# Gate vectors of a two-layer diffusion block: partition sums and spread over partitions in one matrix product instead of two

## What is computed

```
for layer in range(2):
    mod_l = silu(c) @ w_mod[layer] + b_mod[layer]            # latent vectors
    sh1, sc1, g1, sh2, sc2, g2 = split(mod_l, 6)             # 1024 each
    mod_c = silu(c_ctx) @ w_mod[layer] + b_mod[layer]        # context vectors
    y_l, y_c = mixer(LN(x)*(1+sc1)+sh1, ..., w_in, w_out)    # four head groups
    x = post_norm(x, g1 * y_l)                               # LN(ALPHA*x + g1*y)
    x = post_norm(x, g2 * swiglu(LN(x)*(1+sc2)+sh2, w_gate_up, w_down))
    # the same for ctx with cg1, cg2, in layer 0 only
```

## Time and profile before

| | |
|---|---|
| runs of the kernel before | 1733.26, 1728.02, 1728.55 us |
| median | 1728.55 us |
| span of the profiled execution | 1726.8 us |
| PE busy | 1648.3 us (95%) |
| POOL, DVE, ACT busy | 853.3, 826.3, 454.1 us |
| granted TensorE clock, 40 slices | 9 in each of them |

### The profile page before, as it was taken

The page is one execution under the profiler, slowest core; times in us unless marked ns, Lnnn a source line. Parts: engine busy times, 40 slices in busy tenths (PEclk is TensorE's granted clock), DMA queues, the critical chain, the costliest instruction groups (busy, mean ns, idle before and its releaser), DMA issues. The chain is left out here.

```text
span 1726.8 us, 23654 instructions
## 1 busy us (share of the span) xinstructions
PE 1648.3 (95%) x9480; PEld 1391.7 (81%) x9480; DVE 826.3 (48%) x1236; ACT 454.1 (26%) x945; POOL 853.3 (49%) x840
## 2 busy tenths in 40 slices
PE   6999999999899999999999999999999999999997
PEld 4877866767899987899998788786768888688885
DVE  4353254647772415444445684635477421520048
ACT  5511465423500021100003164126433300210021
POOL 4443143623464443544444581523475577587772
PEclk9999999999999999999999999999999999999999
DMA  9212043311353312244642120210013542233321
GB/s 359 76 50 73 2 130 129 109 57 53 98 159 98 110 43 67 64 144 120 198 159 76 67 74 25 73 50 8 26 52 98 147 146 92 92 98 98 98 85 49
DMA packets 157010, 161.98 MB, mean 94 GB/s; under 512 B 6382, under 2 KB 111966, under 8 KB 156646
## 3 DMA queue, kind: packets, MB, share of 16 engines
q1 hardware_dynamic: 136566, 121.40, 22.8%
q10 hardware_dynamic: 20336, 39.08, 6.9%
HBM read 158.36 MB, written 2.10 MB: 93 GB/s over the span
## 5 line engine op out<-in xcount | busy, mean ns | idle before, releaser
L675 POOL TENSOR_SCALAR ring_hi<-stage 128x512 fp32r<-128x512 f32 x352 | 247.9, 704 | 621.4 <-PE ps L745 595.0
L678 POOL TENSOR_TENSOR ring_lo<-stage,ring_hi 128x512 fp32r<-128x512 f32 x352 | 490.0, 1392 | 29.4
L743 PE MATMUL ps<-act_hi,ring_hi 128*128 128x384 f32 (+2 forms) x1088 | 379.9, 349 | 0.0
L745 PE MATMUL ps<-act_hi,ring_lo 128*128 128x384 f32 (+2 forms) x1088 | 378.3, 348 | 0.0
L744 PE MATMUL ps<-act_lo,ring_hi 128*128 128x384 f32 (+2 forms) x1088 | 378.2, 348 | 0.0
L743 PE MATMUL ps<-ring_hi,act_hi 128*128 128x512 f32 (+1 forms) x700 | 280.7, 401 | 11.6 <-DVE act_lo L1872 5.4
L745 PE MATMUL ps<-ring_hi,act_lo 128*128 128x512 f32 (+1 forms) x700 | 273.3, 390 | 0.0
L744 PE MATMUL ps<-ring_lo,act_hi 128*128 128x512 f32 (+1 forms) x700 | 273.1, 390 | 0.0
L745 PEld LDWEIGHTS ps<-act_hi,ring_lo 128*128 128x128 f32 x1088 | 204.6, 188 | 13.2
L743 PEld LDWEIGHTS ps<-act_hi,ring_hi 128*128 128x128 f32 x1088 | 204.7, 188 | 13.0
L744 PEld LDWEIGHTS ps<-act_lo,ring_hi 128*128 128x128 f32 x1088 | 204.7, 188 | 12.9
(11 more groups left out here) (258 smaller groups left out, 2123.3 us busy)
## 6 DMA issues: line engine op xcount, KB each, us to landing
stage<-in_w_gate_up_dram SPq DMA_DIRECT2D x88, 512.0 KB, 5.1
mod_stage<-in_w_mod_dram ACTq DMA_DIRECT2D x56, 512.0 KB, 4.4
stage<-in_w_in_dram SPq DMA_DIRECT2D x18, 1024.0 KB, 5.0
stage<-in_w_down_dram SPq DMA_DIRECT2D x16, 1024.0 KB, 4.9
stage<-in_w_mod_dram SPq DMA_DIRECT2D x12, 1024.0 KB, 5.2
start_mod<-in_w_mod_dram SPq DMA_DIRECT2D x8, 1024.0 KB, 12.3
stage<-in_w_down_dram SPq DMA_DIRECT2D x8, 768.0 KB, 4.4
stage<-in_w_out_dram SPq DMA_DIRECT2D x16, 256.0 KB, 4.5
```

The lines of the kernel that those rows point to most:

```text
L675: nc.gpsimd.tensor_scalar(hi_, stage[:, par, j * 512:(j + 1) * 512], 1.0, 0.0, ALU.mult, ALU.add).then_inc(w_hi, 1)
L678: nc.gpsimd.tensor_tensor(lo_, stage[:, par, j * 512:(j + 1) * 512], hi_.bitcast(F32), ALU.subtract).then_inc(w_ready, 1)
L743: nc.tensor.matmul(o, a_hi, b_hi, start=first, stop=False)
L745: return nc.tensor.matmul(o, a_lo, b_hi, start=False, stop=last)
```

## The change

The accumulators are no longer summed into rows first. `mod_gates` multiplies 128 x 128 ones (`ones` read 128 times) with the accumulator itself: each of the 128 output rows is then the sum over partitions. For layer 0's modG a column `pick_gate` takes the place of the ones; it picks the stream's partial sums and row 2, into which SP brings the bias. For the others DVE adds the bias, once the last part is in, to one partition (0 or 32) of the accumulator (L2062 of the new kernel), from `bias_row`, which SP fills behind units 1 and 2 of `gate_up`.

The modC accumulators are now `bc` itself; those of modG are a new tile, `gate_keep`. The products of L815 and L821, ACT's copies L1413, `sel`, `pick` and the semaphores `gate_summed` and `gate_row_ready` are gone, with the waits for them. PE waits for `ffn_mod_used` (or `gate_keep_in` and `fill_read`) ahead of `mod_gates` instead.

```diff
             def gate_bias(l, seg, i):
 
-                b, m = MOD_BLOCKS[seg][i], GATE_NO[(l, seg, i)]
-                if m >= 2:
-                    sp.wait_ge(gate_out, gates_before(m - 1))
-                sp.dma_start(mod_row[2:3, m % 2, :], b_mod[l:l + 1, b * 512:(b + 1) * 512]).then_inc(bias_row_in[m % 2], 16)
+                b = MOD_BLOCKS[seg][i]
+                src = b_mod[l:l + 1, b * 512:(b + 1) * 512]
+                if (l, seg) == (0, "modG"):
+                    sp.wait_ge(fill_read, 2 * (4 + i) + 2)
+                    sp.dma_start(gate_keep[2:3, i, :], src).then_inc(gate_keep_in, 16)
+                    return
+                if seg == "modC":
+                    sp.wait_ge(ring_used, SLOT0[(l, "wout")] + 8)
+                if (l, seg) != (0, "modC"):
+                    sp.wait_ge(ffn_mod_used, ffn_units((0, 0) if seg == "modG" else (0, 1)))
+                sp.dma_start(bias_row[32 * i:32 * i + 1, :], src).then_inc(bias_row_in[i], 16)
...
+                        if l == 0 and i == 2:
+                            for n in range(2):
+                                gate_bias(l, "modG", n)
...
+                        if f in (1, 2) and seg == "gu0":
+                            gate_bias(l, "modC", f - 1)
+                        elif f in (1, 2) and l < DEPTH - 1:
+                            gate_bias(l + 1, "modG", f - 1)
...
-            def fill_gates(i):
-
-                pe.wait_ge(fill_read, 2 * len(FILL))
-                nc.tensor.matmul(ps[0:2, 4 + i, :], pick_row[:, :], fill_acc[:, i, :], start=True, stop=True).then_inc(gate_summed, 1)
-
-            def gate_sums(item, acc, bank):
-
-                n = streams_of(item)
-                for o in range(n):
-                    mm = nc.tensor.matmul(ps[0:2, bank, :], pick[:, o, :], acc[:, o, :], start=(o == 0), stop=(o == n - 1))
-                mm.then_inc(gate_summed, 1)
-
             def mod_gates(l, seg, bank):
 
+                if (l, seg) == (0, "modG"):
+                    pe.wait_ge(fill_read, 2 * len(FILL))
+                    pe.wait_ge(gate_keep_in, 32)
+                elif seg == "modG":
+                    pe.wait_ge(ffn_mod_used, ffn_units((l - 1, 1)))
+                else:
+                    pe.wait_ge(ffn_mod_used, ffn_units_to((l, 0), FFN_MODS[(l, 0)].index((l, seg, 1))))
                 for i in range(2):
-                    m, n = GATE_NO[(l, seg, i)], GATE_OUT[(l, seg, i)]
-                    pe.wait_ge(gate_row_ready, m + 1)
-                    pe.wait_ge(bias_row_in[m % 2], 16 * (m // 2 + 1))
+                    n = GATE_OUT[(l, seg, i)]
                     for o in range(streams_of((l, seg, i))):
                         if n + o >= 2:
                             pe.wait_ge(gate_read, n + o - 1)
-                        nc.tensor.matmul(ps[:, bank + (n + o) % 2, :], sel[:, o:o + 1].to_broadcast([3, P]), mod_row[:, m % 2, :],
+                        add_up = pick_gate[:, o:o + 1] if (l, seg) == (0, "modG") else ones[:, :]
+                        part = gate_keep[:, i, :] if seg == "modG" else bc[:, o, i * 512:(i + 1) * 512]
+                        nc.tensor.matmul(ps[:, bank + (n + o) % 2, :], add_up.to_broadcast([P, P]), part,
                                          start=True, stop=True).then_inc(gate_out, 1)
...
-                def sums():
-
-                    for n, item in enumerate(FFN_MODS[(l, fh)]):
-                        if item in GATE_NO:
-                            pe.wait_ge(ffn_mod_used, ffn_units_to((l, fh), n))
-                            gate_sums(item, mod_acc_ffn[:, ffn_acc((l, fh), n), :, :], 6 + item[2])
...
                         need(pe, "hid_ready", l, (fh + 1) * HALF)
-                        sums()
                         for t in late:
...
-                            pe.wait_ge(gate_row_ready, GATE_NO[(l, "modC", 1)] + 1)
                             mod_gates(l, "modC", 6)
...
-            def gate_rows(item, bank):
-
-                m = GATE_NO[item]
-                if m >= 2:
-                    act.wait_ge(gate_out, gates_before(m - 1))
-                act.wait_ge(gate_summed, m + 1)
-                a.activation(mod_row[0:2, m % 2, :], ps[0:2, bank, :], ACT.Copy).then_inc(gate_row_ready, 1)
...
+                        to = fill_acc[:, n % 2, :] if n < 4 else gate_keep[:, n - 4, :]
+                        a.activation(to[:, h * 256:(h + 1) * 256], ps[:, 7, 256:512], ACT.Copy).then_inc(fill_read, 1)
...
-                    gate_rows((l, "modC", i), 6 + i)
                 down_hi(l, 0)
                 gate_half(l, 1)
                 if l < DEPTH - 1:
-                    for i in range(2):
-                        gate_rows((l + 1, "modG", i), 6 + i)
+                    act.wait_ge(ffn_mod_used, ffn_units((l, 1)))
                     load_layer(l + 1)
...
-                    acc = mod_acc_ffn[:, ffn_acc(half, n), :, :]
+                    acc = ffn_acc_tile(half, n)
...
+                    if part == 3 and item in GATE_NO:
+                        link(ins)
+                        r, n_s = slice(32 * item[2], 32 * item[2] + 1), streams_of(item)
+                        dve.wait_ge(bias_row_in[item[2]], 16 * (BIAS_ROWS.index(item[:2]) + 1))
+                        ins = v.tensor_tensor(acc[r, 0:n_s, :], acc[r, 0:n_s, :],
+                                              bias_row[r, :].unsqueeze(1).to_broadcast([1, n_s, 512]), ALU.add)
                     done(ins, "ffn_mod_used")
...
-            done(v.reduce_sum(pick_row[:, :], ident[:, :].rearrange("p (j o) -> p o j", j=4)[:, 0:2, :], AX), "start_set")
+            link(v.reduce_sum(pick_row[:, :], ident[:, :].rearrange("p (j o) -> p o j", j=4)[:, 0:2, :], AX))
+            done(v.tensor_tensor(pick_gate[:, :], pick_row[:, :], ident[:, 2:3].to_broadcast([P, 2]), ALU.add), "start_set")
...
                 up_half(l, 0)
-                dve.wait_ge(gate_summed, GATE_NO[(l, "modC", 1)] + 1)
                 down_low(l, 0)
                 up_half(l, 1)
-                if l < DEPTH - 1:
-                    dve.wait_ge(gate_summed, GATE_NO[(l + 1, "modG", 1)] + 1)
                 down_low(l, 1)
```

More of the change, by code:

```diff
@@ L292, in build @@
         c_ready = sem("c_ready")
-        N_CONST = 4
+        N_CONST = 3
         def tiles_of(l):
@@ L481, in build, with ffn_acc_tile @@
         FILL = [(0, "modB", i) for i in range(4)] + [(0, "modG", i) for i in range(2)]
-        def summed_wait(e, item):
-            if item in COL_NO:
-                e.wait_ge(col_out, COL_NO[item] + 1)
-            else:
-                e.wait_ge(gate_summed, GATE_NO[item] + 1)
-        def ffn_acc(half, n):
-            items = FFN_MODS[half]
-            return n % 3 if half == (0, 1) else 0 if items[n][1] != "modC" else 1 + items[n][2]
+        def ffn_acc(half, n):
+            return sum(item in COL_NO for item in FFN_MODS[half][:n]) % 3
+        def ffn_acc_tile(half, n):
+            l, seg, i = FFN_MODS[half][n]
+            if seg == "modC":
+                return bc[:, :, i * 512:(i + 1) * 512]
+            if seg == "modG":
+                return gate_keep[:, i:i + 1, :]
+            return mod_acc_ffn[:, ffn_acc(half, n), :, :]
+        BIAS_ROWS = [(0, "modC"), (1, "modG"), (1, "modC")]
         def ffn_sum_chunk(half, n):
@@ L619, in _ @@
             sp.dma_start(rope_grid[:, :, :, :], tab["rope_grid"]).then_inc(const_in, 16)
-            sp.dma_start(sel[:, :], tab["sel"]).then_inc(const_in, 16)
             for l, seg in ORDER:
                 u0 = UNIT0[(l, seg)]
-                if seg == "gu0":
-                    for i in range(2):
-                        gate_bias(l, "modC", i)
-                if seg == "gu1" and l < DEPTH - 1:
-                    for i in range(2):
-                        gate_bias(l + 1, "modG", i)
                 if seg in MOD_BLOCKS:
                     for i, b in enumerate(MOD_BLOCKS[seg]):
-                        if seg == "modG":
-                            gate_bias(l, seg, i)
                         for h in range(2):
@@ L1061, in fourier @@
                 tiles = tiles_of(l)
-                if l == 0:
-                    for i in range(2):
-                        fill_gates(i)
                 need(pe, "g_ready", l, 1)
@@ L1068, in fourier @@
                 for n, t in enumerate(tiles):
-                    if l == 0 and 2 <= n < 4:
-                        pe.wait_ge(gate_row_ready, GATE_NO[(0, "modG", n - 2)] + 1)
                     if n >= 4:
@@ L1627, in fourier @@
                 need(act, "values_done", l, len(attn_pairs(l)))
-                if l == 0:
-                    for i in range(2):
-                        gate_rows((0, "modG", i), 4 + i)
                 for n, t in enumerate(tiles):
@@ L2071, in ffn_terms @@
                 for u, n, item, part in FFN_WHEN[half][f]:
-                    acc = mod_acc_ffn[:, ffn_acc(half, n), :, :]
+                    acc = ffn_acc_tile(half, n)
```

(12 more changed lines are left out.)

16 lines of the change are left out of this document (7 added, 9 removed).

## The result

The changed kernel ran at 1713.62 us in the median (1712.04, 1712.76, 1714.49, 1715.95), the kernel before beside it at 1730.15; the ratio is 0.9893 with a 95% interval of 0.9876 to 0.9911, so 1.1% faster: 18 us by the ratio, 16.5 between the two medians, where 10.4 was forecast. The forecast time was 1718.1 with a range from 1715.5.

The account below looks back on a forecast made before the run. PE was taken to set the pace, other engines waiting for it. Four stalls, 10.59 us, less 0.18 at the start, gave 10.41: span 1716.4, plus 1.75 for the median, 1718.1 us; range 1715.5 to 1722.8.

Parts of the forecast that it names:

- The four stalls: PE's sums ahead of layer 0's Fourier group (A) and in down (B, C, D): 10.59 us go; all going, chance 0.73.
- the products that stay: mod_gates' 24 products, now with 128 rows instead of 3: rows fed make no difference, price 0.
- the bound for cheaper products: mod_gates: if the 28 ns between product durations are real, 24 x 0.028 = 0.7 us is won.
- a rival at 0.04: Whole kernel: SP's free queue or cheaper products give 2 us on top, 1716.1; chance 0.04.
- The extra microsecond at D: Start of down(1,0): about 1 us more than at C, because DVE held hs_lo back for gate_summed.
- Place A covered by DVE: Fourier group meets a DVE not ready, 1.81 us back; in the rival of a partial gain, 1720.9, chance 0.14.
- more from SP: SP's queue, freed of bias rows ahead of gate_up's weights: priced 0, upper bound some 2 us; rival's chance 0.04.
- Bias adds: Six adds on DVE, behind a chunk's terms: at most 6.0 us of DVE, price 0.
- the cover: DVE's idle time behind the adds, waiting for ACT's SiLU: 8.4 us in the mean, five times the largest add.
- The rival that adds and splits hold each other: DVE's adds and POOL's weight splits stall each other: up to 7.8 us, 1725.9; chance 0.07, shared with half the gain.
- The start: One more DVE instruction ahead of start_set, on which PE's first product waits: 0.18 us lost, bounds 0 and 0.3.
- Its base, 1728.55: Starting point of the forecast: the profiled span of 1726.8 us, with the runs' median 1.75 above it.

Follow-up runs that it names:

- d_sums_wait: Changed kernel with the sums over partitions issued again only at the start of down(1,0), DVE's low part waiting for them; one run, 1715.29 us.
- three_rows: Changed kernel with mod_gates feeding only partitions 0 to 2 of the accumulators, so gate values differ; 1723.16 us, 0.9947 of the kernel before.
- before_128_rows: Kernel before, sums kept, with mod_row and sel on 128 partitions (zeros but for three), same result; 1727.66 us, 0.9971 of the kernel before.
- sums_back: Changed kernel with the products of L815 and L821 issued again at all four places, nobody reading or waiting; 1723.59 us, 0.9952 of the kernel before.
- sp_as_before: Changed kernel with bias rows sent ahead of gate_up's weights, behind the old waits; 1716.21 us, 0.9906 of the kernel before.
- adds_x4: Changed kernel with each of DVE's six bias adds issued four times; 1714.94 us, 0.9903 of the kernel before.
- start_free: Changed kernel with pick_gate computed ahead of the Fourier group's unfolding instead of in the chain before start_set; 1713.50 us, 0.9893 of the kernel before.
- halves_apart: Changed kernel with mod_gates' products in two portions, a chunk of large products apart; 1716.04 us, 0.9907 of the kernel before.
- d_sums: Changed kernel with the sums over partitions issued again only at the start of down(1,0), nobody waiting for them; one run, 1717.77 us.
- three_rows_modc0: Changed kernel with three rows fed in mod_gates of layer 0 modC alone; one run, 1713.75 us.

## Why the prediction was wrong, point by point

The four stalls that it counted were right within 0.3 us. The step that failed was the price of 0 for the products that stay: three rows or 128 made a difference, in waits (1.5 us) and in the clock granted behind these products (4 to 5 us in the traces), where the bound for cheaper products was 0.7 us, a rival at 0.04 went to 2, and the clock stood nowhere.

- **The four stalls**: right. Forecast 1.81, 3.72, 2.01, 3.05, measured 1.80, 3.74, 2.03, 2.75: 10.3 for 10.6. The extra microsecond at D was the wait for `gate_summed` (1.07, d_sums_wait); 0.23 of it came back because the first low part took 1.18 us, where its row had 0.78.
- **The products that stay**: here it failed, twice. The prediction said "Rows fed make no difference of which the trace knows; I take 0", from the durations of one product, 620 and 592 ns. The duration is the same: the medians are 588 ns with three rows and 592 with 128, so the 28 ns between the means weren't real. The nearest row, L821, had 128 rows but weights of two columns. And a duration does not hold what it costs to get to a product: with three rows the weight loads around the products wait 1.5 us more (three_rows, 5.8 us again), and the bound of 0.7 fell short of it. And behind these products the granted clock fell to half in the kernel before, 1.7 us each time, which was neither term nor rival. three_rows and before_128_rows show both from either side. Their size is less sure: by the mean clock 7 us of the gain are clock, of which the traces place 4 to 5 right behind `mod_gates`; feeding 128 rows to the kernel before gave 3 us of clock, feeding three to the changed one took 8. A third of the 7 or so is not placed, and the traced executions mostly had a higher clock than the others of their kernel.
- **Place A covered by DVE, or more from SP**: neither that can be told. sums_back gives the 1.80 back, sp_as_before nothing clear of the scatter.
- **Bias adds**: priced at 0.75 us for one stream and 1.5 for two, they took 0.98 to 1.65 and 1.22 to 2.19; the cover held (adds_x4), as did POOL's. The rival that adds and splits hold each other was right on the holding and wrong on the price. The traces agree with the Trainium skill's rule (SBUF — State Buffer, "SBUF: two separate sides") that the prediction told: four adds of four ended 0.52 to 0.54 us behind POOL's instruction. The low part at D fits it too (POOL's split ends at 1453.21 + 1.30 = 1454.51, the low part at 1455.05). The same would explain the 0.8 us in retention: the unfolding of 1.75 us ends at 342.80, 0.54 behind a split that ends at 342.26, and that of 1.09 at 339.38, 0.53 behind POOL's shorter instruction that ends at 338.85. Both traces of before have the 1.75 us, neither of after has, and before_128_rows, which but for a few zeros set at the start is the kernel before up to there, hasn't either. It goes with the moment, not with the change, and as a cause it is argued, not shown: no run takes POOL's work away.
- **The start**: 0.18 lost was forecast; PE's first product comes at 6.66 us in the trace before and at 6.96 in the one after, but in the two traces the changed kernel is 0.4 us ahead by 26 us all the same. The transfers there move by as much from run to run, and start_free shows no difference.
- **The range**: it ended where the sum's own terms ended. Its base, 1728.55, lay low besides: beside the changed kernel the kernel before had 1730.15, which would have made the forecast 1719.7 and the miss larger. Its 1 us for the median was too little as well: the kernel before scatters from 1728.0 to 1738.9, in good part with the clock.

Open: why three rows let the clock fall at one place and not at another, and where the falls lie that halves_apart has more of. PE was busy in the whole of every window shown behind `mod_gates`, at 1.2 GHz for a part of some and at 2.4 in all of others. The Trainium skill (TensorE: Matmul & The Clock Gate, "Part 1: The HAM clock gate (the "warmup" mystery)") says that the clock is set by how busy PE has been; the busy time of the profile does not tell these windows apart. The number of rows fed ahead of them tells more: a fall at 12 of 16 places with three rows, at none of 36 with 128.

## What to carry to other kernels

Price a product that stays, too, when its operands change shape: read the windows right behind it with the granted clock, not only its duration. At four places two or four fp32 products with three rows cost this kernel nothing in duration, 1.5 us in waits and some us in clock (3 by before_128_rows, 8 by three_rows); feeding all 128 partitions, even with zeros (before_128_rows), was 5 us faster with the same result. A broadcast and a sum over partitions are one product with ones, and a wait on a copy's semaphore can cost an engine more than the product (1.07 of 2.77 us at D).

## What the runs showed of the hardware that was not expected

- With three rows fed at all four places of `mod_gates`, three of the four had the clock at 1.2 GHz right behind, in each of four traces (two of before, two of three rows); with 128 rows none in nine traces; with three rows at one place only, none in one.
- An add of 512 columns on one partition that began while POOL worked on a weight tile ended 0.52 to 0.54 us after POOL's instruction, in four of four cases, and so took 0.98 to 1.65 us.
- Behind a large product, one with another number of rows or columns of weights starts later: at place D of d_sums the sum with two columns starts 1459.07 - 1458.75 = 0.32 us behind, where the large ones start at 0.23, and in three_rows_modc0 the first product with three rows 632.78 - 632.46 = 0.32 us behind. Over the four places the waits of the weight loads are 5.8 us with three rows, 5.7 with 64, and 4.3 or 4.4 with 128.
